# An HGRN kernel's tile products: level by level in seven visits, keys raised block by block

## What is computed

```python
def _hgrn2_scan(q, log_f, k, v, s0):
    ...
    b = jnp.cumsum(log_f.astype(f32).reshape(bt, nc, c, n_heads, kd), axis=2)
    decay = jnp.exp(jnp.where(causal, b[:, :, :, None] - b[:, :, None, :], -jnp.inf))
    attn = jnp.einsum("bcihk,bcijhk,bcjhk->bcijh", qc, decay, kc)
    o_intra = jnp.einsum("bcijh,bcjhv->bcihv", attn, vc)
    contrib = jnp.einsum("bcjhk,bcjhv->bchkv", kc * jnp.exp(b[:, :, -1:] - b), vc)
```

## Time and profile before

| | us |
|---|---|
| median of 3 runs | 3013.67 (3011.49 to 3014.42) |
| profiled execution | 3011.8 |
| its span, first to last instruction | 3010.0 |
| TensorE busy | 2976.2 (99%) |
| VectorE busy | 1752.1 (58%) |
| ScalarE busy | 1353.3 (45%) |
| GpSimd busy | 942.1 (31%) |

### The profile page before, as it was taken

How to read it: one execution, slowest core, us unless ns; L and a number is a source line. 1 busy time by engine, 2 the same in 40 slices (tenths; PEclk the granted TensorE clock), 3 DMA queues, 4 the chain that set the end, 5 groups by cost and what they waited for, 6 DMA issues and landing times. The chain is left out here.

```text
span 3010.0 us, 57468 instructions
## 1 busy us (share of the span) xinstructions
PE 2976.2 (99%) x22229; PEld 2830.4 (94%) x22229; DVE 1752.1 (58%) x3005; ACT 1353.3 (45%) x2650; POOL 942.1 (31%) x1086
## 2 busy tenths in 40 slices
PE   7999999999999999999999999999999999999999
PEld 5899999999999999999999999999999999998887
DVE  4646757568568576685784633344377454555554
ACT  6446455455554554555645542212243232234443
POOL 0024445246245353462353520000214343340110
PEclk9999999999999999999999999999999999999999
DMA  7723122122132221221222325442311322227652
GB/s 275 251 77 100 42 78 86 42 78 82 46 99 63 70 88 49 79 79 49 78 77 64 121 91 152 141 126 84 126 42 49 87 65 78 74 65 247 201 183 104
DMA packets 294016, 300.29 MB, mean 100 GB/s; under 512 B 13240, under 2 KB 254768, under 8 KB 293808
## 3 DMA queue, kind: packets, MB, share of 16 engines
q1 hardware_dynamic: 247968, 230.17, 24.7%
q10 hardware_dynamic: 45840, 67.27, 7.1%
HBM read 247.93 MB, written 49.46 MB: 99 GB/s over the span
## 5 line engine op out<-in xcount | busy, mean ns | idle before, releaser
L889 PE MATMUL bank<-h_hi,w_hi 128*128 128x384 f32 x2496 | 863.7, 346 | 0.0
L889 PE MATMUL bank<-h_hi,w_lo 128*128 128x384 f32 x2496 | 836.2, 335 | 0.0
L889 PE MATMUL bank<-h_lo,w_hi 128*128 128x384 f32 x2496 | 835.3, 335 | 0.0
L889 PEld LDWEIGHTS bank<-h_hi,w_hi 128*128 128x128 f32 x2496 | 468.9, 188 | 12.7 <-issue 7.3
L889 PEld LDWEIGHTS bank<-h_lo,w_hi 128*128 128x128 f32 x2496 | 469.3, 188 | 0.6
L889 PEld LDWEIGHTS bank<-h_hi,w_lo 128*128 128x128 f32 x2496 | 468.5, 188 | 0.0
L2033 POOL TENSOR_TENSOR kq<-kq,fg 128x384 f32<-128x384 f32 x288 | 289.6, 1035 | 163.4 <-PE bank L1025 131.8
L1562 DVE SCALAR_TENSOR_TENSOR acc<-bank,taps,acc 128x372 f32<-128x372 f32 (+5 forms) x512 | 249.2, 508 | 68.4 <-ACT acc L1189 57.0
L1277 ACT ACTIVATE cumb<-cumb,tok_g 128x128 f32<-128x128 f32 x576 | 176.0, 389 | 71.4 <-POOL cumb L1994 71.4
L2440 PE MATMUL bank<-a_hi,v_hi 128*128 128x384 f32 x480 | 161.0, 335 | 2.6 <-DVEq L3231 1.9
L1530 DVE TENSOR_TENSOR w_lo<-raw,w_hi 128x1024 fp32r<-128x1024 f32 x104 | 140.5, 1351 | 38.3 <-ACT w_hi L1170 38.3
(11 more groups left out here) (389 smaller groups left out, 6899.5 us busy)
## 6 DMA issues: line engine op xcount, KB each, us to landing
raw<-in_w_in SPq DMA_DIRECT2D x104, 512.0 KB, 4.1
raw<-in_ffn_w SPq DMA_DIRECT2D x78, 512.0 KB, 5.7
cumb<-cum_scratch SPq DMA_DIRECT2D x72, 512.0 KB, 6.0
ada_late<-in_ada_w SPq DMA_DIRECT2D x8, 2048.0 KB, 9.3
raw_d<-in_ffn_w SPq DMA_DIRECT2D x32, 512.0 KB, 5.3
small<-gate_scratch ACTq DMA_DIRECT2D x72, 192.0 KB, 2.4
hid_scratch<-small SPq DMA_DIRECT2D x20, 576.0 KB, 3.6
s_sum<-hid_scratch ACTq DMA_DIRECT2D x53, 192.0 KB, 3.6
```

The lines of the kernel that those rows point to most:

```text
L889: last = pe.matmul(out, w[i][:, k, :], h[:, k, blk(hb)], start=(k == 0 and j == 0), stop=(k == KT - 1 and j == 2))
```

## The change

The 24 steps are grouped by level: BURSTS says before which eighth of which unit a visit comes (16 is the end of unit 1, 29 is five eighths into unit 3, and so on). There are seven visits, the first with levels 0 and 1, each other with one level's three blocks. A visit can stand inside a unit's accumulation. GpSimd follows the list UPS of levels and blocks without slots and waits block by block, at level 7 in the order 0, 2, 1. There are three key buffers, one per block; the third lies in hs_f[:, 3:6]. ScalarE's copies are spread by KA_EARLY (at the start of a slot) and KA_LATE (behind conv_tanh of the slot, before b_evac). VectorE's blends stand in the slots of MERGES, and the join of slot 5 moves from behind the taps to before them. The first turns of keys wait for their own block alone.

```diff
-def steps_in(slot):
-    return [i for i in (2 * slot, 2 * slot + 1) if 0 <= i < NSTEP]
+BURSTS = {16: (0, 1), 29: (2,), 42: (3,), 55: (4,), 68: (5,), 80: (6,), 92: (7,)}
+KA_EARLY = {1: [(1, 0), (1, 1), (1, 2)], 2: [(2, 0)], 3: [(2, 1), (2, 2)], 4: [(3, 0), (3, 1)], 5: [(3, 2)],
+            6: [(4, 1)], 7: [(5, 0)], 8: [(5, 2)]}
+KA_LATE = {5: [(4, 0)], 6: [(4, 2)], 7: [(5, 1)]}
+UPS = [(lv, b) for lv in range(1, LEVELS + 1) for b in ((0, 2, 1) if lv == LEVELS else range(NB))]
+MERGES = {2: (0, 1), 4: (2,), 5: (3,), 7: (4,), 9: (5,)}
+KEEPS = {10: [(6, 2)], 12: [(7, 1), (7, 2)]}
...
+        ka.append(hs_f[:, 3:6, :].rearrange("p c n -> p (c n)"))
...
                 for k in range(KT):
+                    if between is not None and k > 0:
+                        levels_at(g, KT * between + k)
...
+            def levels_at(g, at):
+
+                for lv in BURSTS.get(at, ()):
+                    for b in range(NB):
+                        level_step(g, lv, b)
...
             def hgrn(g, k):
-                for i in steps_in(k):
...
+                levels_at(g, KT * (k + 1))
                 for i in turns_in(k):
                     kind, b = TURNS[i]
                     if i == 0:
-                        pe.wait_ge(up_ready.sem, up_ready.at(g, LEVELS * NB))
+                        pe.wait_ge(lv_ready.sem, lv_ready.at(g, NSTEP))
+                    if i < 3:
+                        raised(pe, g, LEVELS, b)
...
+            def gather_keys(g, lv, b):
+
+                if lv == 1:
+                    act.wait_ge(q_ready, g * 3 + 3)
+                else:
+                    raised(act, g, lv - 1, b)
+                s = 1 << (lv - 1)
+                act.activation(ka[b][:, :].rearrange("p (n two s) -> p n two s", two=2, s=s),
+                               pairs(0, 3, s, b * BW, BW), ACT.Copy).then_inc(ka_ready.sem, 1)
...
                     if k > 0 and (k - 1) // NB in CONV_TILES:
                         b_th_free(g, k - 1)
                         conv_tanh(g, k - 1)
+                    hgrn_late(g, k)
                     if k == 12:
                         load_states(g)
                     b_evac(g, k)
...
-                if k in JOINS and k <= 4:
+                if k in JOINS and k <= 5:
                     join_decays(g, k)
...
-            def hgrn(g, k):
-                for i in steps_in(k):
-                    lv, b = level(i)
-                    if lv == 0:
-                        continue
+            def hgrn(g):
+                for lv, b in UPS:
+                    wait(lv_ready, g, step(lv, b) + 1)
...
+                    else:
+                        raised(pool, g, lv - 1, b)
+                    if lv in (2, 3, 4, 6):
+                        wait(decay_ok, g, {2: 1, 3: 2, 4: 3, 6: 4}[lv])
```

More of the change, by code:

```diff
@@ L64 @@
 ACT_ROUND, DVE_ROUND, DT_ACT, DT_DVE = 10, 99, 6, 16
-def level(i):
-    return i // NB, i % NB
-def steps_in(slot):
-    return [i for i in (2 * slot, 2 * slot + 1) if 0 <= i < NSTEP]
+BURSTS = {16: (0, 1), 29: (2,), 42: (3,), 55: (4,), 68: (5,), 80: (6,), 92: (7,)}
[5 more added lines that the diff above has]
+KEEPS = {10: [(6, 2)], 12: [(7, 1), (7, 2)]}
 def turns_in(slot):
@@ L690, in mixers @@
     hs_loaded, decay_ok = sem("hs_loaded"), Count(sem("decay_ok"), 4)
-    up_ready = Count(sem("up_ready"), LEVELS * NB)
+    up_ready = Count(sem("up_ready"), len(UPS))
     ka_ready = Count(sem("ka_ready"), IN_BLOCK * NB)
@@ L700, in mixers, with step, raised @@
     hrstd_ok, o_final, o_stored, soh_stored = sem("hrstd_ok"), sem("o_final"), sem("o_stored"), sem("soh_stored")
+    def step(lv, b):
+        return lv * NB + b
+    def raised(eng, g, lv, b):
+        eng.wait_ge(up_ready.sem, up_ready.at(g, UPS.index((lv, b)) + 1))
     def parts_at(k):
@@ L874, in _, with project @@
         def _(pe):
-            def project(g, t, b, hb, cols_n=P):
+            def project(g, t, b, hb, cols_n=P, between=None):
                 i, _, n = tile(g, t)
@@ new lines, in levels_at, with level_step @@
+            def levels_at(g, at):
+                for lv in BURSTS.get(at, ()):
+                    for b in range(NB):
+                        level_step(g, lv, b)
+            def level_step(g, lv, b):
+                i = step(lv, b)
+                if lv == 0:
+                    pe.wait_ge(q_ready, g * 3 + 1)
+                elif lv <= IN_BLOCK:
+                    pe.wait_ge(ka_ready.sem, ka_ready.at(g, i - NB + 1))
+                else:
+                    raised(pe, g, lv - 1, b)
+                if b == 0:
+                    if lv == 1 or lv == 4:
+                        pe.wait_ge(ms_read, g * NB + (2 if lv == 1 else 3))
+                    elif lv == 3 or lv == 5:
+                        pe.wait_ge(v_kept, g * NB + (2 if lv == 3 else 3))
+                    elif lv > IN_BLOCK:
+                        pe.wait_ge(lv_merged.sem, lv_merged.at(g, 1 if lv == 6 else 5))
+                for j in range(CB):
+                    c = b * CB + j
+                    s = 1 << (lv - 1) if lv else 0
+                    w = max(BS, s)
+                    for t in range(P // w):
+                        rows = slice(w * t, w * (t + 1))
+                        out = lv_out(lv, b)[rows, j * w:(j + 1) * w]
+                        own = slice(c * P + w * t, c * P + w * (t + 1))
+                        other = slice(c * P + w * (t ^ 1), c * P + w * ((t ^ 1) + 1))
+                        if lv == 0:
+                            last = pe.matmul(out, k_sum[:, own], q_t[:, own], start=True, stop=True)
+                        elif lv <= IN_BLOCK:
+                            last = pe.matmul(out.rearrange("p (n two s) -> p n two s", two=2, s=s),
+                                             ka[b][:, j * P + w * t:j * P + w * (t + 1)],
+                                             pairs(1, 2, s, c * P + w * t, w), start=True, stop=True)
+                        else:
+                            last = pe.matmul(out, (kf_t, kb_t)[t % 2][:, own], (qf_t, qb_t)[t % 2][:, other],
+                                             start=True, stop=True)
+                last.then_inc(lv_ready.sem, 1)
@@ L1142, in _ @@
                 for k in range(SLOTS):
-                    project(g, 6 + k // NB, k % NB, b_tile(k)[1])
+                    project(g, 6 + k // NB, k % NB, b_tile(k)[1], between=k)
                     if k == 0:
@@ L1150, in _ @@
             for k in range(8 * NB):
-                project(g, 6 + k // NB, k % NB, k % NB)
+                project(g, 6 + k // NB, k % NB, k % NB, between=k)
                 if k == 0:
@@ L1300, in ssd_rstd, with hgrn_late @@
                 act.activation(rstd, rstd, ACT.Exp, scale=-0.5).then_inc(rstd_ok, 1)
+            def gather_keys(g, lv, b):
+                if lv == 1:
+                    act.wait_ge(q_ready, g * 3 + 3)
+                else:
+                    raised(act, g, lv - 1, b)
+                s = 1 << (lv - 1)
+                act.activation(ka[b][:, :].rearrange("p (n two s) -> p n two s", two=2, s=s),
+                               pairs(0, 3, s, b * BW, BW), ACT.Copy).then_inc(ka_ready.sem, 1)
+            def hgrn_late(g, k):
+                for lv, b in KA_LATE.get(k, ()):
+                    gather_keys(g, lv, b)
             def hgrn(g, k):
@@ L1308, in hgrn @@
                                       ).then_inc(hs_loaded, 16)
-                for i in steps_in(k):
-                    lv, b = level(i)
-                    if lv == 0 or lv > IN_BLOCK:
-                        continue
[L1313 to L1325, removed]
+                for lv, b in KA_EARLY.get(k, ()):
+                    gather_keys(g, lv, b)
+                for lv, b in KEEPS.get(k, ()):
+                    wait(lv_ready, g, step(lv, b) + 1)
                     w = 1 << (lv - 1)
@@ L1689, in join_decays @@
                 if k == 4:
-                    wait(up_ready, g, NB)
+                    raised(dve, g, 1, NB - 1)
                 for lv in range(lo, hi):
@@ L1703, in hgrn @@
             def hgrn(g, k):
[L1704 to L1708, removed]
+                for lv in MERGES.get(k, ()):
+                    wait(lv_ready, g, step(lv, NB - 1) + 1)
                     out = at_in[:, :].rearrange("p (c i) -> p c i", i=BS)
@@ L1879, in _ @@
                     b_evac(g, k)
-                    if k in JOINS and k > 4:
+                    if k in JOINS and k > 5:
                         join_decays(g, k)
@@ L2010, in ssd @@
                     sum_squares(g, 2)
-            def hgrn(g, k):
[L2013 to L2016, removed]
+            def hgrn(g):
+                for lv, b in UPS:
+                    wait(lv_ready, g, step(lv, b) + 1)
+                    if lv == 1:
+                        pool.wait_ge(q_ready, g * 3 + 3)
+                    else:
+                        raised(pool, g, lv - 1, b)
+                    if lv in (2, 3, 4, 6):
```

(7 more changed lines are left out.)

## The result

The changed kernel takes 3031.21 us (median of 4 runs, 3028.19 to 3032.99) against 3013.99: a ratio of 1.0056 with a 95% interval of 1.0044 to 1.0068. It is 17 us slower. The forecast was 3028, in a range of 3006 to 3041. The profiled execution is one of 3030.25 us with a span of 3028.5, 18.5 more than before.

What follows compares the result with a forecast made beforehand. TensorE's queue was taken as the bound. A gain of 10.4 us against waits of 8.0 (a), 11.2 (b) and 6.3 (c) made it 15.1 us slower, about 3028 us, in a range of 3006 to 3041.

Steps and rivals of the forecast that it cites:

- What bounds: Up to about 1820 us, time is what TensorE's queue takes, one group every 202.4 us.
- Gain of fewer visits: TensorE's visits to the tile products, twelve becoming seven: about 1.3 us a group gained, bounds 1.0 and 1.6.
- (a): At level 2's visit TensorE waits 1.0 us for the third block's key, in all eight groups; bounds 0 and 1.4.
- the lock rival: GpSimd's next multiplication waits out VectorE's whole join: level 2's wait 1.4 us, level 3's visit later, 3031 us; 13%.
- (b): At level 4's visit TensorE waits 1.6 us for the third key, copied behind unit 5's tanh, in seven groups.
- The floor of 0.8: Even with an idle VectorE, TensorE waits 0.8 us for level 4's third key.
- (c): TensorE waits for banks that VectorE frees, 0.5 us before unit 6 and 0.4 at unit 11, in seven groups.
- one rival: VectorE becomes the bound, with every contended price at its upper end: 3041 us; 12%.
- The third buffer: The third key buffer takes away a wait that hid behind others: worth nothing.
- The last group: No tanh of this kind stands ahead of level 4's copy, so no such wait; its stage no slower than before.

Runs made afterwards that it cites:

- single edits: Each alone on the changed kernel: level 4's third key copied ahead of the tanh, 3021.38 us; slot 5's join behind the taps, 3023.42; level 2's visit later, 3031.68.
- the first two together: Changed kernel with level 4's third key copied ahead of the tanh and slot 5's join behind the taps: 3020.53 us, ratio 1.0021.

## Why the prediction came out right, point by point

**What bounds.** Right: TensorE is still busy for 98% of the span, and what a group lost are waits in its queue.

**Gain of fewer visits.** Predicted 1.3 us a group with bounds 1.0 and 1.6. Without their waits the eight visits of a group (the turn of v alone, the six-block visit, five of 0.99, level 7's) cost 0.33 + 1.80 + 5 x 0.99 + 1.40 = 8.5 us, where the twelve had cost 10.1: 1.6. The six-block visit and those of three blocks were priced right (1.76 and 1.01 predicted, 1.80 and 0.99 measured). The sum was low because 5 x 0.34 - 0.36 took all old visits at 0.76, and the second and third had cost 0.79 and 0.84 and the last two, with level 7, 1.02 and 1.05: 0.66 more in all, the turn of v left aside. Level 7's new visit, 1.40 where 1.01 was taken, gives back part of it. A visit in the middle of a unit costs what one at its end does (0.99 for levels 3 and 6).

**(a) Level 2's keys.** Predicted 1.0. Its visit costs 1.89 to 2.25 us in seven groups and 1.61 in the last, so it waited 0.9 to 1.3 (1.2 in six of them), and 0.6. GpSimd's six multiplications took 8.38 us, where the earlier trace rows gave 8.15; the extra is in the first one, 1.53 for 1.25 us. The one beside the join took 2.30 us, as before the change (2.31). So the 0.4 us that the lock rival added did not come.

The traces show why. The join starts while a multiplication runs and ends 1.22 us after it, in both kernels (291.67 to 292.89 before, 294.16 to 295.38 after); the next multiplication, started by then, ends 1.04 and 1.05 us after the join. The Trainium skill (SBUF — State Buffer, "SBUF: two separate sides") has the shared port pair held for a whole instruction, while the other engine waits. The traces agree, before the change too. By an estimate from these ends the join's own work is 1.22 us; of the 1.52 in the earlier trace rows 0.3 were such a wait, and of the 2.09 now 0.9. The prediction took 1.52 for the join's own length, and its blocked multiplication for one as long as join and multiplication together, which would be 1.5 + 1.2 = 2.7 and was 2.31. The lock rival named 3031 us, the time that was measured, but this is chance: (a) is not 1.4, and level 3's visit is not late (0.99 us, no wait).

**(b) Level 4's third key.** The mechanism was right, the term too small: 1.6 predicted, at most 2.0, and 2.45 measured, more in one group, and none in the last, as predicted. The step that failed is "join 0.71": the two joins of slot 5 took 1.92 us at 311.31, on GpSimd's level 3 (308.31 to 314.02). Before the change this join had fallen where GpSimd had just finished (0.79 at 314.19). I gave the silu a contended price and the join beside it an uncontended one. The error is larger than the total shows: the chain was taken to start at U6, 311.8 us here, and VectorE came to the blend 0.9 us earlier, at 310.94. The floor of 0.8 was measured to 0.03 once that join was out of the way.

**(c) Banks.** 0.9 predicted, nothing measured. The chain was right, its place in the sum was not. While TensorE waits for level 2's keys GpSimd runs dry, so VectorE's next instructions were the cheap ones (weights 1.22, silu 0.55 us, at 306.89 and 308.02), and the long wait at level 4 gave VectorE the rest. With level 2's visit later they took 2.04 and 1.27, and unit 6 did wait. I had seen this as an argument against one rival and not used it in my own sum. The waits for banks came out as the others were taken away: that before unit 6 (0.7 us over the pace) without level 2's wait, those before units 7 (0.5) and 11 (0.8) without level 4's.

**The third buffer** was taken at nothing and is worth 9 us; the kernel has it, so the sum was not touched.

**The last group** gained 0.8 us; by the prediction's terms 0.3.

In all, the gain and (c) were mis-sized in the opposite direction to (a) and (b). A group was to lose 2.2 us, as -1.3 + 1.0 + 1.6 + 0.9, and lost 2.1 as -1.6 + 1.2 + 2.5 + 0: over 1 us of error each way. The direction and the leading wait were foreseen; that the total came within a few microseconds is luck. (By its own sum the median was to be 3013.67 + 15.1 = 3028.8, where the prediction says about 3028.) The seven full groups come to 7 x (1.2 + 2.5 - 1.6) = 14.7 us of loss, with (a) as it was in six of them; the remaining one, the second, waited 0.3 less there and lost 0.3 inside unit 2 instead. The third lost another 0.3 in its stage A, the lower clock in one group adds 1.3, the last group gives 0.8 back, and 2.9 us lie outside the groups in that one execution. That is 18.4 of the 18.5.

## What to carry to other kernels

Before work is moved in one queue, follow each moved instruction's own queue: what cost most of the time was one 0.5 us copy placed behind a tanh, which waited for VectorE's taps, with which the copy had nothing to do. Waits in series hide one another: (c) was invisible until (a) or (b) was taken out, single edits regained 10, 8 and 0 us and the first two together 11, so the sum of the waits that a profile shows is no forecast of what their removal brings. And where an engine that is 58% busy on average has a stretch without gaps, move its deferrable work out of that stretch first; here that was worth 8 us with no instruction fewer.

## What was not expected of the hardware

A wait of TensorE of 1.8 us (two buffers) to 2.5 us was now and then followed by a few microseconds at the lower clock: in one group of seven in the changed kernel, two of seven with the later visit, three with two buffers, and in no group of the profiles whose waits in the groups were 1.4 us or shorter. Each cost 1.3 to 1.6 us. So a wait of that length is dearer than its length; how it comes that most groups with the same wait keep the clock, no run here tells.
